# Three panels instead of two on the unnormalised operand behind a norm, with the norm's sum in strips and one small product moved

## The reference, cut to what matters

```
rmsnorm(x, w)  = x * rsqrt(mean(x*x) + 1e-6) * w
first block, twice:
  x = x + 0.5 * swiglu(rmsnorm(x), gate, up, down)        # width 2816
  x = x + mixer(rmsnorm(x))                               # w_in, three recurrences, w_out
  x = x + 0.5 * swiglu(rmsnorm(x), gate, up, down)
x = rmsnorm(x, norm_final)
second block, once:
  h = x + rmsnorm(mixed(rmsnorm(x)) @ w_o, g_post_mix)
  f = square(relu(rmsnorm(h) @ w_up)) @ w_down            # width 4096, the MLP
  h = h + rmsnorm(f, g_post_mlp)
  gate = sigmoid(rmsnorm(h) @ w_ple_gate + b)
  h = h + rmsnorm(gate * (p @ w_ple_in), g_post_ple)      # p: 256 tokens x 256
```

## Time and profile before

| what | value |
|---|---|
| time, median of 3 runs (lowest to highest) | 1914.84 us (1914.05 to 1917.64) |
| the profiled execution | 1914.54 us, its span 1912.7 us |
| granted TensorE clock over the span | 0.977 |
| PE busy | 1794.1 us (94%) |
| DVE busy | 1090.4 us (57%) |
| ACT busy | 917.1 us (48%) |
| POOL busy | 176.9 us (9%) |
| chain that ended last, by engine | PE 81%, DVE 9%, ACT 5%, POOL 2%, issue 2% |
| HBM traffic | 287.75 MB read, 151 GB/s over the span |

### The profile page before, as it was taken

The page is one execution under the profiler, slowest core; times in us unless marked ns, Lnnn a source line. Parts: engine busy times, 40 slices in busy tenths (PEclk is TensorE's granted clock), DMA queues, the critical chain, the costliest instruction groups (busy, mean ns, idle before and its releaser), DMA issues.

```text
span 1912.7 us, 34097 instructions
## 1 busy us (share of the span) xinstructions
PE 1794.1 (94%) x15120; PEld 1729.0 (90%) x15120; DVE 1090.4 (57%) x1231; ACT 917.1 (48%) x966; POOL 176.9 (9%) x120
## 2 busy tenths in 40 slices
PE   8999987899999999999789999999999989899997
PEld 7999987799999999998779999889897779899986
DVE  6544788464446544688556445654465456655555
ACT  6343674453345334476444344544444454544444
POOL 0000071000000000052000000774000000000000
PEclk9999998899999999999899999999999999999999
DMA  7555442135555555453035555456254514445541
GB/s 258 177 184 191 144 134 88 46 122 186 178 183 169 177 178 193 148 162 117 19 102 176 178 187 187 142 186 206 93 170 160 176 39 162 138 159 191 180 160 39
DMA packets 206530, 290.99 MB, mean 152 GB/s; under 512 B 4560, under 2 KB 170576, under 8 KB 206128
## 3 DMA queue, kind: packets, MB, share of 16 engines
q1 hardware_dynamic: 205936, 287.04, 46.3%
q0 software_dynamic: 448, 1.77, 0.3%
HBM read 287.75 MB, written 1.05 MB: 151 GB/s over the span
## 4 chain that ended last, share of the span: by engine, by line
PE 81%; DVE 9%; ACT 5%; issue 2%; POOL 2%; DMA 0%; SPq 0%; ACTq 0%; DVEq 0%
PE colb L788 52%; PE acc L788 26%; PE aux L788 2%; DVE w_lo L1527 2%; ACT w_hi L1177 2%; POOL arena L657 1%; DVE arena L1732 1%; DVE u L1587 1%; DVE x L1630 1%; DVE u L1645 1%; DMA raw<-ffn_gate 0%; DVE op_lo L1593 0%; POOL arena L658 0%; ACT arena L1490 0%; DVE arena L1790 0%
## 5 line engine op out<-in xcount | busy, mean ns | idle before, releaser
L1527 DVE TENSOR_TENSOR w_lo<-raw,w_hi 128x2048 fp32r<-128x2048 f32 x271 | 626.0, 2310 | 591.1 <-ACT w_hi L1177 590.5
L1177 ACT ACTIVATE w_hi<-raw 128x2048 fp32r<-128x2048 f32 x271 | 515.8, 1904 | 414.2 <-PE acc L788 230.7
L788 PE MATMUL colb<-u_hi,w_lo 128*128 128x256 f32 x2256 | 295.7, 284 | 5.7 <-DVE w_lo L1527 5.7
L788 PE MATMUL colb<-u_hi,w_hi 128*128 128x256 f32 x2256 | 298.1, 285 | 1.7 <-ACT u_hi L1287 0.9
L788 PE MATMUL colb<-u_lo,w_hi 128*128 128x256 f32 x2256 | 295.0, 284 | 0.0
L788 PEld LDWEIGHTS colb<-u_hi,w_lo 128*128 128x128 f32 x2256 | 282.3, 193 | 6.5 <-DVE w_lo L1527 6.5
L788 PEld LDWEIGHTS colb<-u_hi,w_hi 128*128 128x128 f32 x2256 | 283.4, 193 | 3.1 <-issue 1.5
L788 PEld LDWEIGHTS colb<-u_lo,w_hi 128*128 128x128 f32 x2256 | 282.2, 193 | 0.0
L788 PE MATMUL acc<-op_hi,w_hi 128*128 128x256 f32 x1328 | 203.9, 286 | 12.4 <-ACT op_hi L1299 8.1
L788 PE MATMUL acc<-op_hi,w_lo 128*128 128x256 f32 x1328 | 201.0, 284 | 0.2
L788 PE MATMUL acc<-op_lo,w_hi 128*128 128x256 f32 x1328 | 200.4, 284 | 0.0
(11 more groups left out here) (298 smaller groups left out, 1725.6 us busy)
## 6 DMA issues: line engine op xcount, KB each, us to landing
raw<-w_in SPq DMA_DIRECT2D x78, 1024.0 KB, 5.1
raw<-ffn_gate SPq DMA_DIRECT2D x44, 1024.0 KB, 5.3
raw<-ffn_up SPq DMA_DIRECT2D x44, 1024.0 KB, 5.3
raw<-ffn_down SPq DMA_DIRECT2D x44, 1024.0 KB, 4.9
raw<-w_up SPq DMA_DIRECT2D x16, 1024.0 KB, 5.4
raw<-w_down SPq DMA_DIRECT2D x16, 1024.0 KB, 5.0
raw<-w_out SPq DMA_DIRECT2D x8, 1024.0 KB, 4.9
raw<-w_ret_out SPq DMA_DIRECT2D x8, 1024.0 KB, 4.9
```

What stands on the lines that cost most here:

```text
L788: return pe.matmul(o, a, b, start=start, stop=stop, skip_group_check=True)
L1177: act.activation(split_view(w_hi, r), raw[:, p % RAW_SLOTS, 0:r["kt"] * r["nc"]], ACT.Copy)\
L1527: tt(split_view(w_lo, r), raw[:, p % RAW_SLOTS, 0:r["kt"] * r["nc"]], split_view(w_hi, r).bitcast(F32), ALU.subtract).then_inc(sem("w_lo_r ...
```

## The change

`EARLY` is 3: three column panels behind each of the nine norms run on the unnormalised operand, and VectorE multiplies three banks by `rstd`. ScalarE makes `op_hi` itself from `x` with the gain as its scale (two 128x256 instructions a chunk); VectorE's `x_gained` is gone, and `op_lo` and `u32` are made from `x` with `scalar_tensor_tensor`, tile by tile. VectorE updates the first chunk of `x`, makes `w_lo` of the first panel there, updates the other three, and only then makes `op_lo`. The whole `fill` stands at the second panel, behind `w_hi` and `w_lo` of the panel two further on. The first panel (and the first on `u`) does its products in the order high x high, low weight, low operand. Except at the first norm, the sum of squares stands behind the first panel, as 8 products whose stationary operand is 32 columns of ones, in four strips of the output's partitions; ScalarE copies the strips, and one product with 128 columns, inside the second panel, adds them. `p @ w_ple_in` becomes a panel of a new kind, `P`, between the norm of mixing's result and its use; it goes to three `colb` banks and `aux` and is copied to SBUF (`ple_e`). In the MLP every row panel stands one column panel later. `x_update("post")` goes chunk by chunk. `p` is fetched at the start of the second block.

```diff
-EARLY = 2
+EARLY = 3
@@ ffn
+                if i == 1:
+                    step("op_hi", r=todo)
                 if i:
                     step("op_lo", r=todo)
-                u = panel(kpn(up)[:, :, i * PC:(i + 1) * PC], KD, PC, "A", u_op, [], by="dve",
+                u = panel(kpn(up)[:, :, i * PC:(i + 1) * PC], KD, PC, "A", u_op, [("u_ready", 4 * f)], by="dve",
...
-                r = operand(hid[:, len(ops) % 2, :], [("dve_evac", u["n"])])
+                r = operand(hid[:, len(ops) % 2, :], [("dve_evac", u["n"])] + [("panel_used", u["p"] + EARLY - 1)] * (i == 0))
@@ second_block
+            step("load_p")
...
+                if i == 3:
+                    p_op = operand(p32[:, :, :].rearrange("p a b -> p (a b)"), [("p_loaded", 16)])
+                    step("op_hi", r=p_op)
+                    step("op_lo", r=p_op)
                 row_gemm_panel(ap["w_o_2"][0], i, rs[i], i == 0, i == 3)
             n = norm_sum("acc")
+            p_op["panel"] = len(panels)
+            resident(ap["w_ple_in_2"][0], op_tiles(p_op), [("op_ready", p_op["r"] + 1)], ple_e)
             x_update("post", norm=n, gain="g_post_mix_2")
...
-            step("load_p")
             f = pre_norm("g_pre_mlp_2", 0)
-            todo = None
+            todo = []
             for i in range(16):
...
+                if i == 2:
+                    for o in todo:
+                        step("op_hi", r=o)
+                        step("op_lo", r=o)
                 step("relu2", r=len(ops), evac=n_act)
-                if i == 1:
-                    step("op_hi", r=todo)
-                    step("op_lo", r=todo)
-                if i:
-                    row_gemm_panel(ap["w_down_2"][0], i - 1, todo, i == 1, False)
+                if i >= 2:
+                    row_gemm_panel(ap["w_down_2"][0], i - 2, todo.pop(0), i == 2, False)
...
-            row_gemm_panel(ap["w_ple_in_2"][0], 0, p_op, True, True)
@@ tensor, gemm
+                elif r["kind"] == "P":
+                    pe.wait_ge(sem("w_lo_ready"), p + 1)
+                    pe.wait_ge(sem("op_ready"), op_ready)
+                    for i, o in enumerate([colb[:, (r["c"] + i) % 3, :] for i in range(3)] + [aux[:, :]]):
...
+                            pe.wait_ge(sem("rstd_ready"), r["norm"])
...
-                    for part in range(3):
+                    for part in (0, 2, 1) if r.get("gained") or r.get("fresh") else (0, 1, 2):
...
+                            if part == 1 and kk == 2 and r.get("half") == 1 and r["norm"] > 1:
+                                parts_sum(r)
...
                 last.then_inc(sem("panel_used"), 1)
+                if r.get("gained") and r["norm"] > 1:
+                    parts(r)
+
+            def parts(r):
+                pe.wait_ge(sem("sq_ready"), 4 * r["norm"])
+                for kk in range(KD):
+                    g = slice(32 * (kk % 4), 32 * (kk % 4) + 32)
+                    last = mm(aux[g, 0:T], ones[:, 0:32], sq[:, kk, :], kk < 4, kk >= 4)
+                last.then_inc(sem("norm_parts"), 1)
+
+            def parts_sum(r):
+                pe.wait_ge(sem("parts_copied"), r["fill"]["n"] - 1)
+                mm(aux[:, T:2 * T], ones, rstd[:, :]).then_inc(sem("norm_summed"), 1)
@@ scalar, panel
                 if r.get("scaled"):
-                    fill(r["fill"], r["half"])
                     split_hi_to(r["p"] + 2)
+                    if r["half"] == EARLY - 2:
+                        fill(r["fill"])
...
+                if r["kind"] == "P":
+                    for i in range(4):
...
+                        act.activation(r["dst"][:, 2 * i:2 * i + 2, :].rearrange("p a b -> p (a b)"),
+                                       colb[:, (r["c"] + i) % 3, :] if i < 3 else aux[:, :], ACT.Copy).then_inc(sem("act_evac"), 1)
+                    return
@@ scalar, norm_sum
+                def high(b):
+                    chunk(b)
...
+                    for t in range(2):
+                        ins = act.activation(gained_chunk(op_hi, r["op"], b)[:, t, :], x[:, 2 * b + t, :], ACT.Copy,
+                                             scale=c(r["gain"], r["at"] + 2 * b + t))
+                    ins.then_inc(sem("g_hi_ready"), 1)
...
+                high(0)
+                square(0)
+                for b in (1, 2, 3):
+                    high(b)
+                split_hi_to(r["panel"] + 1)
+                for b in (1, 2, 3):
+                    square(b)
                 ln_exp_tables()
+                split_hi_to(r["panel"] + 2)
+                act.wait_ge(sem("norm_parts"), r["fill"])
+                act.activation(rstd[:, :], aux[:, 0:T], ACT.Copy).then_inc(sem("parts_copied"), 1)
                 act.wait_ge(sem("norm_summed"), r["n"])
+                rstd_from(rstd[:, :], aux[:, T:2 * T], 1.0 / (32 * D)).then_inc(sem("rstd_ready"), 1)
@@ vector
             def panel(r):
                 split_lo_to(r["p"] + 1)
-                if r.get("scaled"):
-                    fill(r["fill"], r["half"])
+                if r.get("scaled") and r["half"] == EARLY - 2:
+                    split_lo_to(r["p"] + 2)
+                    fill(r["fill"])
...
             def gained(r):
                 for b in range(4):
...
                         update[0](b)
-                    x_gained(r, b)
-                    if b:
-                        g_lo_(r, b - 1)
-                g_lo_(r, 3)
+                    if b == (0 if r["nx"] else 3):
+                        split_lo(panels[n_lo[0]])
+                        n_lo[0] += 1
+                if r["nx"]:
+                    for b in range(4):
+                        g_lo_(r, b)
...
+            def fill(r):
                 dve.wait_ge(sem("rstd_ready"), r["norm"])
                 dve.wait_ge(sem("panel_used"), r["panel"])
+                for i in range(4):
+                    for kk in (2 * i, 2 * i + 1):
+                        ins = stt(u32[:, kk, :], x[:, kk, :], c(r["gain"], r["at"] + kk), rstd[:, :], ALU.mult, ALU.mult)
+                    ins.then_inc(sem("u32_ready"), 1)
+                for i in range(4):
+                    dve.wait_ge(sem("u_hi_ready"), 4 * (r["n"] - 1) + i + 1)
+                    s = slice(2 * i, 2 * i + 2)
+                    tt(u_lo[:, s, :], u32[:, s, :], u_hi[:, s, :].bitcast(F32), ALU.subtract).then_inc(sem("u_ready"), 1)
...
+                        if r["kind"] == "post":
+                            for i in (2 * b, 2 * b + 1):
+                                ins = stt(u32[:, i, :], acc[:, T * i:T * i + T], c(r["gain"], i), rstd[:, :], ALU.mult, ALU.mult)
...
             def ple(r):
                 dve.wait_ge(sem("act_evac"), r["evac"])
-                dve.wait_ge(sem("panel_used"), r["panel"])
...
-                    tt(g, g, bank[b], ALU.mult).then_inc(sem("gated_ready"), 1)
+                    tt(g, g, ple_e[:, 2 * b:2 * b + 2, :].rearrange("p a b -> p (a b)"), ALU.mult)\
+                        .then_inc(sem("gated_ready"), 1)
```

More of the change, by code:

```diff
@@ L281, in panel @@
                 early[0] -= 1
+                fresh[0] = True
+            elif kind != "row":
+                r["fresh"], fresh[0] = fresh[0], False
             if kind != "row":
@@ L312, in wide, with resident @@
             return r
+        def resident(w, xop, ready, dst):
+            nonlocal n_col, n_act
+            r = dict(p=len(panels), src=kpn(w), kt=2, nc=D, kind="P", xop=xop, ready=ready, c=n_col, by="act", dst=dst,
+                     n=n_act + 4)
+            for i in range(3):
+                bank_users.append(("act", n_act + i + 1))
+            n_act += 4
+            n_col += 3
+            r["norm"] = count["norm"]
+            panels.append(r)
+            schedule.append(("panel", r))
+            return r
         def step(name, **more):
@@ L330, in fill, with norm_sum @@
             return count["fill"]
-        def norm_sum(src, next_="x_update"):
+        def norm_sum(src, next_="x_update", **more):
             count["norm"] += 1
-            step("norm_sum", n=count["norm"], src=src, x=count["x"], group=count["group"], next=next_, fill=count["fill"])
+            step("norm_sum", n=count["norm"], src=src, x=count["x"], group=count["group"], next=next_, fill=count["fill"], **more)
             return count["norm"]
@@ L340, in pre_norm @@
             step("gained", gain=gain, at=at, n=count["fill"] + 1)
-            n = norm_sum("x", "fill")
-            f = fill(norm=n)
+            n = norm_sum("x", "fill", gain=gain, at=at)
+            f = fill(norm=n, gain=gain, at=at)
             return f
@@ L798, in gemm @@
                 u_ready, op_ready = ready.get("u_ready"), ready.get("op_ready")
-                if r["kind"] not in ("row", "W") and r["c"] >= 3:
+                if r["kind"] not in ("row", "W", "P") and r["c"] >= 3:
                     col_bank_free(pe, r["c"] - 3)
@@ L860, in gemm @@
                                 pair = (w[:, m_], xo) if r["kind"] == "A" else (xo[:, m_], w)
```

(23 more changed lines are left out.)

110 lines of the change are left out of this document (60 added, 50 removed).

## The result

| kernel | median us (lowest to highest, runs) | against the kernel before, 95% interval |
|---|---|---|
| before | 1914.68 (1912.90 to 1917.64, 9) | |
| changed | 1919.84 (1918.28 to 1922.56, 9) | 1.0028, 1.0019 to 1.0037 |

The account below looks back on a forecast made before the run. TensorE was taken to bound the kernel, 81% of the span, so only its waits could be won. Terms +0.7 - 4.5 + 1.0 + 1.8 + 4.4 - 2.0 = +1.4 us gave 1916 us, range 1904 to 1926.

Parts of the forecast that it names:

- my own case: Whole kernel: the terms as summed, +1.4 us, 1916 us; likeliest case alone 1911 to 1920; chance 0.40.
- First panel, strips, fill, stalls: Behind a feed-forward: first-panel stall 0.7 us, strips 1.2, fill 4.3 after second panel's end (E), fourth-panel stall 1.0, row-panel stall 0.9.
- (c): Strips don't overlap in fours: 3.5 instead of 1.2 us at eight norms, +18, 1934 us; chance 0.08.
- A norm: Each of three norms behind a feed-forward: 4.2 against 5.8 us, taken as -1.5; together -4.5 us.
- MLP: Ahead of the MLP, the first row panel stalls 8.7 us in place of 4.0; +4.4, bounds +2 and +7.
- Mixers: Two mixers: the first panel's gain of 5 us turns to +0.5 each, ScalarE and VectorE bounding; +1.0 us.
- Mixing: Second block's input: the fifth panel's w_hi comes later; +1.8 us, bounds +1.2 and +2.7.
- PLE: Without the small product there, the last column panel ends at 1893.2 instead of 1895.2; -2.0 us.
- Start: First norm: the row panel starts 13.4 us after the second panel's end, at 38.8 instead of 38.05; +0.7 us.
- (a): Queue behind the fill shorter: row stalls 1 us less at seven norms, 3 at the MLP; about 1906; chance 0.22.
- (b): No new stall: 3.5 us won at each of eight norms and the MLP's 4; about 1884; chance 0.06.
- (d): MLP's row stall and the queue longer: +1 us at five norms, +2 at the MLP; 1923; chance 0.24.

Follow-up runs that it names:

- experiment 2: Changed kernel with the MLP's first row panel's op_hi and op_lo made right behind the fill: 1912.45 us, 0.9988 of before.
- 4: Changed kernel with EARLY 2 (two panels), which also puts the fill at the first panel: 1900.56 us, 0.9918 of before.
- 5: Changed kernel, three panels kept, with the fill at the first panel instead of the second: 1906.34 us, 0.9954 of before.
- Experiment 1: Changed kernel with the mixer's preparation moved to the fourth and fifth column panels of the first feed-forward: 1916.44 us, 1.0005 of before.
- 3: Changed kernel with VectorE's fill ahead of w_lo and the first panel on u taking the low weight last: 1908.77 us, 0.9966 of before.
- 6: Changed kernel, three panels, with fill at the first panel, preparation later and the MLP's first op_hi one evacuation sooner: 1899.52 us, 0.9922 of before.
- 7: Changed kernel with two panels and the mixer's preparation later: 1898.82 us, 0.9920 of before.
- 10: Two panels, preparation later, with eight full products of ones instead of strips, copy and adding product: 1905.94 us, 0.9956 of before.
- 11: Two panels, preparation later, with each MLP row panel again directly behind the next column panel: 1907.29 us, 0.9965 of before.
- 12: Two panels, preparation later, with the MLP's first op_hi and op_lo behind the second bank's evacuation: 1899.55 us, 0.9922 of before.
- 8: Two panels, preparation later, with the fill ahead of w_lo on VectorE and the low weight last: 1921.26 us, 1.0030 of before.
- 9: Changed kernel, three panels, with eight full products of ones instead of strips, copy and adding product: 1938.14 us, 1.0121 of before.

## Why the prediction was right, and where it was off

It said 1916 us, 1904 to 1926, with no measurable change the likeliest at 0.38 and slower by over 0.2% at 0.33. Measured: 1919.84, by 0.28% slower. The range holds, and so does my own case's (1911 to 1920); the direction came out one class beyond the one I held likeliest. Most of what is missing between 1.4 us of sum and 5.2 measured is one term, the start. By its own steps:

- **First panel, strips, fill, stalls: right.** The last `op_hi` stretches the first 16 matmuls from 2.08 to 2.84 (0.7 was said, 0.76 is shown). Strips: 1.09 us from the end of the first panel's issue (612.91) to the second panel's start, said 1.2, in bounds of 0 and 3.5. The Trainium skill (TensorEngine Tiling, Key Properties) has a change of mode drain the engine; a quarter of the full form's 3.62 us is 0.91, so by that estimate two changes cost about 0.2 together here. Whether the engine drains no row shows; the price is small either way. (The rival (c) would by its own sum have decided from 1.5 us a norm on, not 1.7.) Fill at E+4.4 (4.3). Fourth panel's stall 1.3 (1.0): its high part ends 3.2 behind the third panel's end, for 1.92. Row panel's 0.5 (0.9). A norm: -1.8 (-1.5).
- **MLP: right.** Wait 8.34, said 8.7; +4.5, said +4.4; experiment 2 shows it to be the queue named. The lower clock cost as said: 3.75 for the 16.
- **Mixers: right in sum,** +0.9, said +1.0, and by the mechanism named: the fifth `w_hi` stands behind the second bank's evacuation, 3.14 us of wait ahead of it. Experiments 4 and 5 show what I had not seen in it, that this wait belongs to the fill's place and can be had back. The +0.8 of the first and the +0.1 of the second differ by the clock behind the same wait of 3.14 (3.21 and 2.14 for 16 matmuls).
- **Mixing +1.0 (said +1.8), PLE -1.3 (said -2.0):** right in sign, 0.7 to 0.8 off, and by luck in opposite directions, so that the sum doesn't show it.
- **Start: the step that failed.** It said that the row panel would follow the second panel's end by 13.4, giving +0.7. It followed by 16.0. I had read VectorE's and ScalarE's queues behind the fill as scaling, silu, `op_hi`, taken from the MLP and the later feed-forwards, and at the start there is one step more, `setup` with a table load: 2.6 us. (In the kernel before, `op_hi` stood ahead of `setup`; the change put it behind.) After the longer wait TensorE ran at the lower clock in this execution and was through with the panel at 50.12, 1.55 later than at the full clock; experiment 2's profile shows that this doesn't always follow. Another 1.3 of the +6.5 is the late DMA, which lies in the spread of 11.1 to 12.9; with the +0.7 that is 6.2 of the 6.5. Experiment 1 takes the step away and finds 13.3.
- **The last norm: +1.6, not said.** Its 16 products took 5.31, at the lower clock for a part of it, after a wait of 2.32, where before they ran in 3.72 after one of 2.31; nothing of the change stands there. After the same 2.32 they took 3.72 in experiments 2 to 7 and 10 to 12 and 5.24 to 5.28 in 1, 8 and 9, in code that is the same there.
- **Rivals.** (a) and (b) are out: the queue was as long as I stacked it. (c) is out: strips overlap. (d), longer row stalls, is about as near in time (1923 was said) as my own 1916, and its stalls at six places weren't found; the queue was longer at one, the start.

What the prediction didn't ask is whether the change was slow by its parts or by their order. It was the order: with the fill placed where `rstd` frees it, the same work runs in 1899. But the third panel, which gives the change its name, is worth nothing (1899.52 with it, 1899.55 without). Of the 16 us that two panels gain over the kernel before, the strips were shown to bear 7; with the whole fill, the later row panels of the MLP are needed too (8.5). Without the strips 8 us are left; what ScalarE's `op_hi`, the moved product and the post norm by chunks have of them was not tested one by one.

## What to carry to other kernels

When work is moved to cover a wait, look at what the waiting engine has done by the time the wait ends: VectorE sat idle for 5 us ahead of `rstd` while a `w_lo` that could not be made yet was queued between `rstd` and the fill. An instruction whose release comes from the engine that you want to keep fed should not stand ahead of the one that feeds it; what is ready early should. And read the queue of each occurrence by itself: the one term that failed was copied from other norms, and the first had a step more.

## What the hardware did that was not expected

- Four strips of 32 columns ran 3.4 times as fast as the full form (16 instructions in 1.07 against 3.62 us by their records), near the four that the count allows, in float32.
- The same swap of two VectorE instructions gave -11 us in one schedule and +22 in the other.
- Strips were worth 18.3 us with three panels and 7.1 with two, for the same instructions at the same places. The time of an instruction on the busiest engine isn't its worth where another chain ends last.
- What clock TensorE had after a wait didn't follow from the wait's length alone. After waits of 5.43, 7.50 and 8.34 us its next 16 matmuls took 3.71 to 3.76 us, and the window behind the 8.34 shows a granted clock of 0.50; after waits of 0.35 to 1.80 they took about 2.15. In between it went either way: after 3.07 and 3.14 they took 3.28 and 3.21 in the changed kernel (granted 0.62 and 0.64), after 3.08 and 3.14 in the rows above 2.14 at 1.00. The 16 products of ones at the end took 3.72 after 2.31 and 5.31 after 2.32. So a long wait that is removed can give back more than its length. Whether one of 2.3 to 3.1 us also makes executions of one kernel differ is not shown, since each kernel has one profile.
